# A mixture-of-experts stage on one Trainium2 core: gates' tables ahead of the row numbers and the first turn, two weight pieces behind a layer's first gather

## What is computed

```python
def moe_ffn(x, w_router, router_bias, w_gate, w_up, w_down):
    x2d = x.reshape(bsz * t, d)
    gates = group_limited_router(x2d, w_router, router_bias)   # two of 16 per token
    y = jnp.zeros((bsz * t, d), jnp.float32)
    for e in range(N_EXPERTS):
        he = jax.nn.silu(x2d @ w_gate[e]) * (x2d @ w_up[e])
        y = y + gates[:, e:e + 1] * (he @ w_down[e]).astype(jnp.float32)
```

## Time and profile before

| | us |
|---|---|
| median of three timed runs | 950.39 (948.04 to 950.72) |
| profiled execution, its own time | 945.88 |
| span of the profiled execution | 944.1 |
| PE busy | 883.0 (94%) |
| DVE busy | 407.5 (43%) |
| POOL busy | 298.5 (32%) |
| ACT busy | 254.1 (27%) |
| mean DMA rate | 289 GB/s |
| weights and other loads by SP's queue | 247.14 MB |

### The profile page before, as it was taken

One profiled execution on the slowest core, in us unless ns is written; L12 is line 12 of the kernel. 1 busy time (PEld: TensorE's weight loads), 2 busy tenths in 40 slices (PEclk: granted clock), 3 DMA queues, 4 the chain that ended last, 5 costly groups with the idle time before them and its releaser, 6 DMA issues.

```text
span 944.1 us, 15539 instructions
## 1 busy us (share of the span) xinstructions
PE 883.0 (94%) x5890; PEld 567.4 (60%) x5890; DVE 407.5 (43%) x928; ACT 254.1 (27%) x473; POOL 298.5 (32%) x220
## 2 busy tenths in 40 slices
PE   6998799889999999999999997998899999989996
PEld 5876668755555555555487766787555555545552
DVE  5997756731111111111659977477311111111126
ACT  5424841301111111111233347412111111111111
POOL 0632436222222222223334324462222222212223
PEclk9999899979999999999999998999799999999999
DMA  9761067799999999997514211678998999999972
GB/s 305 266 250 55 3 257 320 272 416 405 405 407 400 409 406 406 403 393 204 148 26 134 90 55 34 266 281 308 418 398 333 401 407 405 407 409 401 396 174 89
DMA packets 66132, 272.78 MB, mean 289 GB/s; under 512 B 8834, under 2 KB 24354, under 8 KB 40992
## 3 DMA queue, kind: packets, MB, share of 16 engines
q1 hardware_dynamic: 53792, 247.14, 65.7%
q0 software_dynamic: 12288, 24.89, 10.6%
HBM read 256.83 MB, written 21.76 MB: 295 GB/s over the span
## 4 chain that ended last, share of the span: by engine, by line
PE 62%; DVE 16%; DMA 12%; SPq 5%; issue 2%; ACT 1%; POOL 1%; DVEq 0%; POOLq 0%
PE bank L785 25%; PE bank L791 14%; PE bank L445 13%; DMA moew<-in_exp_w_down 8%; DVE bank L1170 6%; SPq L338 4%; DMA w_gate<-in_w_in 2%; PE bank L779 2%; DVE xTl L1139 2%; PE bank L773 2%; PE bank L836 2%; DMA moemem<-x_rows,first_tok 2%; PE bank L832 2%; DVE w_gate L1146 1%; POOL wl L1588 1%
## 5 line engine op out<-in xcount | busy, mean ns | idle before, releaser
L1421 DVE TENSOR_TENSOR moemem<-bank,moemem 64x128 f32<-64x128 f32 x172 | 48.3, 281 | 312.5 <-ACT moemem L1048 309.8
L1641 POOL DMA_INDIRECT moemem<-x_rows,gather_idx x43 | 45.1, 1048 | 283.8 <-DVE moemem L1435 259.8
L785 PE MATMUL bank<-w_up,moemem 128*64 128x256 f32 x1088 | 127.1, 388 | 0.0
L1588 POOL TENSOR_TENSOR wl<-w_gate,wh 128x2048 fp32r<-128x2048 f32 x17 | 78.0, 4593 | 137.7 <-ACT wh L911 98.6
L445 PE MATMUL bank<-xTh,wh 128*128 128x512 f32 (+1 forms) x256 | 100.1, 391 | 11.5 <-DVE xTl L1139 10.2
L785 PEld LDWEIGHTS bank<-w_up,moemem 128*64 128x64 f32 x1088 | 79.7, 140 | 45.1 <-issue 8.5
L1048 ACT ACTIVATE moemem<-bank 64x256 f32<-64x256 f32 x86 | 32.8, 381 | 247.5 <-PE bank L785 247.5
L445 PE MATMUL bank<-xTh,wl 128*128 128x512 f32 (+1 forms) x256 | 94.4, 369 | 0.0
L445 PE MATMUL bank<-xTl,wh 128*128 128x512 f32 (+1 forms) x256 | 94.2, 368 | 0.0
L1635 POOL DMA_INDIRECT y_rows<-moemem,scatter_idx x43 | 69.3, 1612 | 62.6 <-ACT moemem L1053 50.2
L785 PE MATMUL bank<-w_gate,moemem 128*64 128x256 f32 x736 | 83.4, 379 | 1.2 <-DMA w_gate<-in_exp_w_wide 1.2
(11 more groups left out here) (225 smaller groups left out, 1287.4 us busy)
## 6 DMA issues: line engine op xcount, KB each, us to landing
w_up<-in_exp_w_wide SPq DMA_DIRECT2D x24, 2048.0 KB, 28.0
w_gate<-in_exp_w_wide SPq DMA_DIRECT2D x16, 2048.0 KB, 24.6
w_down<-in_exp_w_down SPq DMA_DIRECT2D x16, 2048.0 KB, 24.7
w_down<-in_exp_w_wide SPq DMA_DIRECT2D x8, 2048.0 KB, 33.6
w_gate<-in_exp_w_down SPq DMA_DIRECT2D x8, 2048.0 KB, 36.6
xtok<-in_exp_w_wide SPq DMA_DIRECT2D x8, 2048.0 KB, 24.1
moex<-in_exp_w_wide SPq DMA_DIRECT2D x8, 2048.0 KB, 26.5
moew<-in_exp_w_down SPq DMA_DIRECT2D x8, 2048.0 KB, 31.0
```

The source lines that it names most:

```text
L785: return [pe.matmul(bank[i][CH * n:CH * n + CH, 0:256], x, w[:, 512 * n + 256 * i:512 * n + 256 * i + 256], start=(k == 0), stop=(k == KD ...
L1421: dve.tensor_tensor(he[CH * b:CH * b + CH, P * i:P * i + P], bank[i][0:CH, P * b:P * b + P], silu[:, 256 * i + P * b:256 * i + P * b + P], ...
L1588: pool.tensor_tensor(wl[(n + l) % SLOTS][:, :], wraw[n % 2], wh[(n + l) % SLOTS][:, :].bitcast(F32), ALU.subtract)\
L1641: return pool.indirect_dma_start(to, None, x1_halves[l], bass.IndirectOffsetOnAxis(ap=rows[:, :], axis=0), bounds_check=2 * T - 1, oob_is_ ...
```

## The change

Five moves, the same in each layer:

1. SP holds e1 LOW_K and e2 LOW_K back until the first gather has landed (first_in), where it waited for the logits (lgT_done).
2. TensorE loads 2 chunk starts instead of 6 ahead of the row numbers' products, and none right after them; the others are loaded at the heads of experts 0 to 14, one each.
3. TensorE computes the gates' table ahead of its wait for the first gather and of the turn, where it did so behind them.
4. DVE computes the gates ahead of its wait for the row numbers' products, and writes the row numbers behind them.
5. POOL loads its two chunk starts ahead of its wait for the row numbers, with a wait for start_set.

```diff
@@ SP
                 sp.wait_ge(tr_done, TT * (2 * l + 1))
                 load_expert(l, 1, HIGH_K)
 
-                sp.wait_ge(lgT_done, TT * (l + 1))
+                sp.wait_ge(first_in, 16 * (l + 1))
                 load_expert(l, 1, LOW_K)
                 load_expert(l, 2, LOW_K)
@@ TensorE, route
                 pe.wait_ge(start_set, l + 1)
-                starts = [first_chunk(pe, l, e) for e in range(6)]
+                starts = [first_chunk(pe, l, e) for e in range(2)]
...
                 mm.then_inc(tab_done, 1)
-                starts += [first_chunk(pe, l, e) for e in range(6, 12)]
                 return starts
@@ TensorE, order
                 starts = route(l)
+                late_tables(l)
                 pe.wait_ge(first_in, 16 * (l + 1))
                 turn_gathered(l)
-                late_tables(l)
@@ DVE, route
                 link(dve.tensor_reduce(gt, kk2.rearrange("p r (j e) -> p (r j) e", j=TT), AX.X, ALU.add))
-                dve.wait_ge(tab_done, l + 1)
-                link(dve.tensor_scalar(toki[:, :], bank[3][:, 0:MAXCH], cst[:, K_OFF:K_OFF + 1], None, ALU.add))
-                dve.sem_inc(tab_set, 1)
-
                 link(dve.tensor_tensor(m1, gt[:, 0:TT], gt[:, TT:2 * TT], ALU.add))
...
                 dve.tensor_tensor(hot_gate[:, :, MAXCH:2 * MAXCH], hot_chunk, bc3(gt, MAXCH), ALU.mult)                   .then_inc(rt_late, 1)
+
+                dve.wait_ge(tab_done, l + 1)
+                link(dve.tensor_scalar(toki[:, :], bank[3][:, 0:MAXCH], cst[:, K_OFF:K_OFF + 1], None, ALU.add))
+                dve.sem_inc(tab_set, 1)
@@ POOL
                 gather_rows(l, xg, first_tok).then_inc(first_in, 16)
+                pool.wait_ge(start_set, l + 1)
+                first, end = first_chunk(pool, l, 0), first_chunk(pool, l, E)
                 pool.wait_ge(tab_set, l + 1)
-                first, end = first_chunk(pool, l, 0), first_chunk(pool, l, E)
                 pool.tensor_copy(gather_idx[:, :], toki[:, bass.ds(first + 1, 1)]).then_inc(idx_set, 1)
```

## The result

Over four timed runs each, taken on one chip, the kernel before took 950.46 us (948.04 to 950.72) and the changed kernel 956.12 us (952.48 to 957.14). The ratio is 1.0055, with an interval of 1.0033 to 1.0076: **slower by some 5.2 us**, above the range of the prediction. (The medians themselves lie 5.7 us apart.) The profiled execution took 952.48 us with a span of 950.4 us, against 945.88 and 944.1: 6.3 us more. On either side the profiled execution is no longer than the shortest timed one, so the two can be compared, but what the longer executions spend their time on is not seen.

What follows compares the result with a forecast made beforehand. TensorE and the queue of weights were taken to bound the stages together; +2.1 us (layer 0, stream) + 0 - 0.9 (layer 1, clock) = +1.2 moved the median of 950.39 to 951.6 us, range 947.6 to 955.0.

Steps and rivals of the forecast that it cites:

- Step 1: Entry of the expert stage: the first gather lands 4.7 us after its issue, 3.6 us earlier than now.
- Step 2: Layer 0's weight stream: holding the two pieces delays the stage's end by 2.1 us (1.5 to 2.8); layer 1: 0.
- The landings way: Layer 0's stream: the hold's cost sized by e2 LOW_K landing at 207.2 against 205.7, a delay of 1.5 us.
- Step 3: Tables first on TensorE and DVE: first chunk 1.3 us earlier in layer 0, worth nothing there; 0 in layer 1.
- Step 4: TensorE's granted clock in the entry: it rises earlier, saving 0.9 us in layer 1; swallowed in layer 0.
- Step 5: TensorE's register loads, moved to expert boundaries: cost 0, with a bound of 1 us per layer.
- C: Layer 0's entry: gather not freed, pieces go out only behind it, 5.1 us of delay; +4.2, 954.6 us; 20%.
- A: Layer 0 bound by TensorE: the stream's 2.1 us is hidden and the 1.3 us counts; -2.2, 948.2 us; 20%.
- D: Layer 1's hole in the DMA doesn't take the delay: +2.1 twice - 0.9 = +3.3, 953.7 us; 8%.

Runs made afterwards that it cites:

- the hold alone: The kernel before, with only SP's wait ahead of e1 LOW_K and e2 LOW_K changed to the first gather's landing: 952.88 us, ratio 1.0040.
- one piece held: The changed kernel with e1 LOW_K issued at the old place and only e2 LOW_K held for the first gather: 950.34 us against 949.17, ratio 1.0013.
- the order alone: The changed kernel with the old wait for the logits ahead of e1 LOW_K and e2 LOW_K: 949.7 us against 949.85, ratio 1.0006.
- the hold in layer 1 alone: The kernel before, with e1 LOW_K and e2 LOW_K held for the first gather in layer 1 only: 950.51 us, ratio 1.0000.

## Why the prediction was wrong

The place, the mechanism and the sign of the largest term were right, its size was not, and a term with the wrong sign was set against it: +1.2 was forecast in sum, and some +5.2 measured (+6.3 in the profiled executions).

**Step 1, the first gather: right in kind.** It was to land 4.7 us after its issue. It took 5.4 us in layer 0 and 4.7 us in layer 1; in the hold alone 4.3 and 5.0. The kernels that hold nothing have 7.1 to 8.3 us in layer 0. The rule of the Trainium skill that was weighed ("DMA: Bandwidth & Descriptors", section "Queues, rings and completion order": a whole packet of one queue before the next) would have had the gather gain little from what is queued behind e1 HIGH_K. With both pieces gone it gained 2 to 4 us, so the trace doesn't bear that reading out; with one of the two still there it took 7.8 us and gained none.

**Step 2, what the hold costs the stream: the term that failed, by its size.** The place was right (layer 0, by way of the stream, as stalls of more than 3 us; layer 1 at no cost because of its hole). The forecast size was 2.1 us, from a pause of 2.8 us and landings that gave 1.5. The pause was 4.0 us, and the pieces that ended the stalls came 4.5 us late. Of the 1.2 us between 2.8 and 4.0, 0.7 is the gather's 5.4 instead of 4.7 us, and 0.3 is e1 HIGH_K, issued 3.9 us ahead of the gather and not 3.6, so that it ran dry earlier. Taking the mean with the landings took off another 0.7. The landings way was right for the piece that it looked at: in the two kernels with the hold in the old order, e2 LOW_K landed 1.4 and 2.0 us later than before (the changed kernel's landing isn't recorded). But that isn't the delay that travels on: e2 DOWN, two pieces behind it, was 2.3 and 3.1 us late in the same two. The restart was well read: the first held piece, e1 LOW_K, took 8.2 and 7.6 us there, forecast 7.7. (The 2.0 us that the prediction set beside the 2.7 us comes from a section on transfers that GpSimd issues, and SP issues these pieces.) The other part of the error lies in how the pause reaches the end. The w_down that ends the stalls lands 4.5 us later than before when counted from the gather's issue (187.1 against 182.6), so a little more than the pause; these 0.5 us I can't place. And I took TensorE's wait for moew at 407 as the spot where the delay would come out. It came out 32 to 43 us earlier, at three pieces of another expert. The last of them lands in before 0.15 us ahead of its use and so shows no wait in a list of waits.

**A term that wasn't in the sum: the clock behind the stalls.** After three waits within 13 us TensorE's clock stood at 0.58 and 0.56, and the products there took 1.6 us longer than elsewhere. I counted the stalls of a stream-bound stage as their own length only. The Trainium skill has the effect: "TensorE: Matmul & The Clock Gate", section "HAM oscillation — how this bites in real kernels", tells of products that start at the low clock behind a wait for DMA. The trace agrees for the changed kernel, with single waits of 0.80, 1.85 and 1.89 us, and the run with one piece held shows that it need not happen.

**Step 3, tables first: right.** The first chunk was to start at 198.8, 9.74 us after the gather's issue; it started 9.60 us after it. In layer 1: 9.67 us, forecast 9.79. Pool's copy of the row numbers was to be no later, and is not: the second gather goes out 7.5 us after the first, where it was 8.2. The gain was called swallowed in layer 0, and was: 1.0 of the 1.5 us went to the low clock in the first chunk (step 4), and the 0.5 us that the second chunk still had only made TensorE wait longer for the same pieces.

**Step 4, the clock: wrong.** An earlier rise was to save 0.9 us in layer 1; the measured row has layer 1's stage 0.2 us longer. The granted clock reads 0.69 over 201 to 203 and 0.72 over 679 to 681, so it rose at about 202.2 and 680.1, which is 14.2 and 15.0 us after the gathers' issues; in before it was 13.7 and 14.8 us. The rise did not come earlier with the chunk. As the chunk did start earlier, more of it ran at the low level: the first 64 products took 9.38 and 9.73 us, against 8.37 and 9.55. In layer 0 that gave back 1.0 of the 1.5 us won. What decides the moment of the rise stays open.

**Step 5, register loads: right.** The second and third chunks start 11.61 us apart, and the order alone has a ratio of 1.0006 (0.9988 to 1.0023).

In the profiled executions the 5.1 us between forecast (+1.2) and result (+6.3) are thus 3.6 in layer 0's stage (2.4 of delay and 1.6 of clock, less the 0.4 us wait for moew), 1.1 in layer 1's, and 0.3 in stretches that the change doesn't touch.

**The rivals.** C had the time nearest (954.6 us) and the mechanism half right: its premise, a gather that isn't freed, is false, but what made it costly, pieces that go out so late that the stream loses some 5 us, is nearly what happened with the gather freed (4.0 us of pause, 4.5 at w_down). That it came nearest is to that extent luck. Its condition, "from a gather landing of about 195 us on", was too generous: counted from the entry of before (issue at 189.06), the gather landed at 194.4, and the change lost all the same. A is refuted by the stalls: TensorE doesn't come late enough to hide anything. D is refuted by the hold in layer 1 alone, if narrowly: 1.0000 (0.9981 to 1.0020), where a cost of 2.1 us there would be 1.0022.

## What to carry to other kernels

Where a transfer queue is the limit of a stage, a wait put ahead of its next transfers costs at least the pause until bytes flow again (here 2.5 to 4.0 us for a hold until a gather of 4.3 to 5.4 us has landed), however long before their use the held pieces land; what made it free here was idle DMA time ahead of the next piece without time to spare. A list of waits doesn't show that spare time: compare each piece's landing with its first use, since a piece that lands 0.15 us ahead of it is as binding as one that is waited for. When an experiment is to lighten a stream, look at its GB/s and at the amount of work behind it before its time is read.

## What the runs showed of the hardware

- A gather's time depends on what is queued behind the piece in flight, and not in proportion: in layer 0, 4.3 to 6.1 us with nothing queued at its issue, 7.1 to 7.9 us with one piece queued, 7.1 to 8.3 us with two. In layer 1 it is 4.5 to 5.2, 6.8 to 7.4 and 6.9 to 7.6 us.
- Three waits of 0.8 to 1.9 us in a stretch of dense products were followed by some 4 us at a granted clock of 0.56 to 0.58, which cost about 1.6 us on top of 4.5 us of waits. In one profile of another kernel a single wait of 2.35 us, up to 374.03, came with a clock of 0.60 from 374 to 382; in a third, behind waits of 0.43 and 2.42 us, the clock stayed at 1.00.
- A load of 1024 KB onto 64 partitions gave no relief over one of 2048 KB onto 128: the DMA engines were 1.02 busy at 337 GB/s, and the three such loads took 15.7 to 21.8 us from issue to landing. The same 1024 KB onto 128 partitions landed in 11.2 and 12.6 us (two of the three are recorded) and made the room that was wanted. These times hold the wait behind other pieces too.
